# Turned token blocks leave PSUM by two engines, and the overflow list is made later

## What is computed

```
glog = (hf @ w_group + b_group)                    # 4 groups, the best one is taken
elog_sel = ... the 8 logits of that group
top_p, top_i = lax.top_k(jax.nn.softmax(elog_sel, -1), 2)
comb = one_hot weights (token, expert)
a = einsum("nd,edf->nef", hf, w_gate); u = einsum("nd,edf->nef", hf, w_up)
hid = silu(a) * u * comb
y = einsum("nef,efd->nd", hid, w_down)             # w_gate, w_up 1024 x 256, w_down 256 x 1024, all float32
```

## Time and profile before

| | us |
|---|---|
| median of 3 runs | 1248.11 |
| lowest and highest | 1244.79, 1253.91 |
| the profiled execution | 1250.47 |
| span of its instructions | 1248.6 |
| mean granted clock of TensorE | 0.963 |

### The profile page before, as it was taken

One profiled execution on the slowest core, in us unless ns is written; L12 is line 12 of the kernel. 1 busy time (PEld: TensorE's weight loads), 2 busy tenths in 40 slices (PEclk: granted clock), 3 DMA queues, 4 the chain that ended last, 5 costly groups with the idle time before them and its releaser, 6 DMA issues.

```text
span 1248.6 us, 13186 instructions
## 1 busy us (share of the span) xinstructions
PE 1142.8 (92%) x4510; PEld 491.0 (39%) x4510; DVE 477.0 (38%) x1133; ACT 229.1 (18%) x421; POOL 96.1 (8%) x163
## 2 busy tenths in 40 slices
PE   4899999899689999999959999999969999999983
PEld 0444544445433333333335544544643333333331
DVE  0453232226822333333455231334673333333336
ACT  0523220302220000000023332341240000000001
POOL 4000000004210000000030000000420000000000
PEclk9999999998799999999989999999889999999997
DMA  9966548437859999999751322311556999999962
GB/s 375 382 255 248 211 191 331 185 109 269 340 189 400 367 381 377 376 382 392 288 224 38 119 68 101 102 43 76 202 220 258 400 382 392 385 377 382 384 233 84
DMA packets 50087, 328.31 MB, mean 263 GB/s; under 512 B 6144, under 2 KB 7248, under 8 KB 13312
## 3 DMA queue, kind: packets, MB, share of 16 engines
q1 hardware_dynamic: 43520, 299.92, 61.3%
q0 software_dynamic: 4912, 20.95, 4.4%
q10 hardware_dynamic: 1616, 6.93, 1.5%
HBM read 320.90 MB, written 6.88 MB: 263 GB/s over the span
## 4 chain that ended last, share of the span: by engine, by line
PE 80%; DMA 11%; DVE 4%; ACT 2%; issue 2%; SPq 1%; DVEq 0%; PEldq 0%; ACTq 0%
PE bank L647 36%; PE bank L1018 15%; PE bank L1044 11%; PE bank L1035 9%; DMA ring<-in_w_moe 6%; PE bank L668 3%; DMA ring<-in_w_mod 2%; DMA region<-h_store,toki 1%; PE bank L1001 1%; PE bank L1060 1%; PE bank L1027 1%; DMA ring<-in_w_in 1%; DMA ring<-in_w_out 1%; ACT hT L1393 1%; PE bank L1080 1%
## 5 line engine op out<-in xcount | busy, mean ns | idle before, releaser
L1018 PE MATMUL bank<-ring,region 128*64 128x512 f32 x1024 | 236.4, 605 | 5.7 <-issue 5.5
L1044 PE MATMUL bank<-region 128*128 128x512 f32 x384 | 173.3, 601 | 0.0
L647 PE MATMUL bank<-ring,hT 128*128 128x512 f32 x384 | 171.6, 599 | 1.7 <-DMA ring<-in_w_in 1.7
L1018 PEld LDWEIGHTS bank<-ring,region 128*64 128x64 f32 x1024 | 70.3, 138 | 146.6 <-issue 146.6
L1035 PE MATMUL bank<-ring,region 128*64 128x512 f32 x512 | 117.3, 600 | 7.5 <-DMA ring<-in_w_moe 5.6
L1044 PEld LDWEIGHTS bank<-region 128*128 128x128 f32 x384 | 70.3, 190 | 102.5 <-issue 102.5
L647 PEld LDWEIGHTS bank<-ring,hT 128*128 128x128 f32 x384 | 70.9, 190 | 90.5 <-issue 89.9
L2043 DVE TENSOR_TENSOR region<-bank,region 128x512 f32<-128x512 f32 x128 | 82.4, 686 | 47.3 <-PE bank L1035 47.3
L647 PE MATMUL bank<-ring,region 128*128 128x512 f32 x192 | 88.1, 608 | 6.7 <-DMA ring<-in_w_out 3.2
L647 PE MATMUL bank<-hT,ring 128*128 128x384 f32 x256 | 89.2, 500 | 1.3 <-DMA ring<-in_w_in 1.3
L2039 DVE TENSOR_TENSOR region<-region,bank 128x256 f32<-128x256 f32 x32 | 13.5, 421 | 199.8 <-ACT region L1510 199.8
(11 more groups left out here) (301 smaller groups left out, 971.1 us busy)
## 6 DMA issues: line engine op xcount, KB each, us to landing
ring<-in_w_moe SPq DMA_DIRECT2D x201, 1024.0 KB, 9.1
ring<-in_w_mod SPq DMA_DIRECT2D x48, 1024.0 KB, 9.5
ring<-in_w_in SPq DMA_DIRECT2D x24, 1024.0 KB, 7.8
ring<-in_w_out SPq DMA_DIRECT2D x4, 1024.0 KB, 7.5
ring<-in_w_out SPq DMA_DIRECT2D x8, 512.0 KB, 4.2
region<-gate_store POOLq DMA_DIRECT2D x4, 1024.0 KB, 6.6
region<-in_lnrows POOLq DMA_DIRECT2D x4, 1024.0 KB, 8.5
h_store<-region ACTq DMA_DIRECT2D x6, 512.0 KB, 3.3
```

Source lines behind the costliest of these rows:

```text
L647: ins = pe.matmul(out, lhsT, rhs, start=start, stop=stop, skip_group_check=True)
L1018: ins = pe.matmul(bank[6][u * CAP:(u + 1) * CAP, :], xs[:, k, u * CAP:(u + 1) * CAP], ring[:, u, j, at:at + 2 * DE], start=k == 0, stop=k ...
L1044: ins = pe.matmul(bank[2 * t + y][:, :], cwp[:, t * P:(t + 1) * P], ysb[:, min(t, 1), y * HALF:(y + 1) * HALF], start=False, stop=False, s ...
```

## The change

- PE: the group q = 1 of each block goes to bank 6 or 7 (`bank[6 + s % 2]`) instead of a bank of `pj()`. Block 0 waits there for `tok_sb` (all row numbers made, bank 6 free), block 1 for `diag_ready` (bank 7 free), blocks 2 to 5 for the copy of the block two before.
- DVE copies those groups into `xg`, six a layer; ACT keeps the six groups with q = 0 and the four `qrow` copies. The `diag` products no longer have a wait of their own.
- DVE does these copies right behind `diag_ready` (in layer 0 behind `mod_columns`), then `bring_x(0)`, and only then makes the overflow list. In `bring_x(0)` the two register loads now stand ahead of the waits for `xg_ready` and for its own copies.
- PE's product that spreads the list moves from the end of `gather` to behind the up products of pair 0 and its one `add_input`.
- The loop over the overflow experts uses one semaphore for what were two. The order of its work stays.

```diff
@@ gather (PE)
                     for q in range(2):
-                        b = pj()
+                        if q == 0:
+                            b = pj()
+                        else:
+                            b = bank[6 + s % 2]
+                            if s == 0:
+                                pe.wait_ge(S["tok_sb"], (l + 1) * len(ROW_GROUPS))
+                            if s == 1:
+                                pe.wait_ge(S["diag_ready"], l + 1)
+                            if s >= 2:
+                                pe.wait_ge(S["up_free"], l * SC + s - 1)
                         for k in range(4):
                             ins = pe.transpose(b[:, k * P:(k + 1) * P], xrows[s][:, (4 * q + k) * P:(4 * q + k + 1) * P], ident[:, :])
-                        ins.then_inc(S["pj_ready"], 1)
+                        ins.then_inc(S[("pj_ready", "up_ready")[q]], 1)
                     if s == NT - 1:
-                        pe.wait_ge(S["diag_ready"], l + 1)
...
-                pe.wait_ge(S["list_col"], l + 1)
-                pe.matmul(bank[7][:, 0:3 * MAXL], ones[0:MAXL, :], xdiag[:, :, :].rearrange("p a b -> p (a b)"),
-                          start=True, stop=True, skip_group_check=True).then_inc(S["list_row"], 1)
@@ experts (PE)
                 up_first(0)
                 up_second(0)
                 add_input(l, HIDDEN_SUMS)
+                pe.wait_ge(S["list_col"], l + 1)
+                pe.matmul(bank[7][:, 0:3 * MAXL], ones[0:MAXL, :], xdiag[:, :, :].rearrange("p a b -> p (a b)"),
+                          start=True, stop=True, skip_group_check=True).then_inc(S["list_row"], 1)
                 turn_step(0)
...
-                        pe.wait_ge(X[l]["cw"], i + 1)
+                        pe.wait_ge(X[l]["cw"], i * 4 + 4)
@@ ACT
                 for s in range(SC):
-                    for q in range(2):
-                        free(f(xg[:, 4 * q:4 * q + 4, s * P:(s + 1) * P], pj()[:, :].rearrange("p (a c) -> p a c", a=4), ACT.Copy))
+                    free(f(xg[:, 0:4, s * P:(s + 1) * P], pj()[:, :].rearrange("p (a c) -> p a c", a=4), ACT.Copy))
@@ DVE
                 dve.sem_inc(S["diag_ready"], 1)
 
+                if l == 0:
+                    mod_columns(1, 2)
+                for s in range(SC):
+                    dve.wait_ge(S["up_ready"], l * SC + s + 1)
+                    dve.tensor_copy(xg[:, 4:8, s * P:(s + 1) * P], bank[6 + s % 2][:, :].rearrange("p (a c) -> p a c", a=4)).then_inc(S["up_free"], 1)
...
                 def bring_x(i):
                     off = [dve.value_load(offi[0:1, bass.ds(i * G + u, 1)], min_val=0, max_val=NS) for u in range(G)]
+                    if isinstance(i, int) and i == 0:
+                        dve.wait_ge(S["xg_ready"], l + 1)
+                        dve.wait_ge(S["up_free"], (l + 1) * SC)
...
+                bring_x(0)
                 ob = lambda a: a[0:MAXL, :].unsqueeze(1).broadcast_to([MAXL, MAXJ, NE])
...
                 dve.sem_inc(S["list_col"], 1)
 
-                if l == 0:
-                    mod_columns(1, 2)
...
-                dve.wait_ge(S["xg_ready"], l + 1)
-                bring_x(0)
                 dve.wait_ge(S["list_row"], l + 1)
```

More of the change, by code:

```diff
@@ L347, in backbone_step @@
             "fin_state",
-            "h_out", "tok_ps", "tok_sb", "rt_ready", "list_col", "list_row", "gexp_in", "gexp", "assign", "ranks", "slots", "lists", "diag_ready", "xg_ready",
+            "h_out", "tok_ps", "tok_sb", "rt_ready", "list_col", "list_row", "up_ready", "up_free", "gexp_in", "gexp", "assign", "ranks", "slots", "lists", "diag_ready", "xg_ready",
             "cw_ready", "cw_step", "comb_done", "acc_done", "xs_ready", "gu_ready", "sg_ready", "hid_ready", "ht_ready", "ht_sb", "ya_ready", "yb_ready", "ya_sb", "yb_sb",
@@ L358, in backbone_step @@
         landed = [[sem(f"landed{u}_{j}") for j in range(3)] for u in range(G)]
-        X = [{n: sem(f"x{n}{l}") for n in ("l0", "l1", "l2", "xs", "u0", "gu", "sg", "hid", "ht", "hts", "yb", "yas", "ybs", "cw", "ws", "cb")} for l in range(DEPTH)]
+        X = [{n: sem(f"x{n}{l}") for n in ("l0", "l1", "l2", "xs", "u0", "gu", "sg", "hid", "ht", "hts", "yb", "yas", "ybs", "cw", "cb")} for l in range(DEPTH)]
         SMALL = [(small[:, :], A["small"]), (tiny[:, :], A["tiny"])]
@@ L368, in backbone_step @@
         PJ_FRONT = [1, 1]
-        N_PJ_L0 = PJ_FRONT[0] + H * (PJ_HEAD + MV) - MV + 2 * NT + 2 * SC + 4
+        N_PJ_L0 = PJ_FRONT[0] + H * (PJ_HEAD + MV) - MV + 2 * NT + SC + 4
         PJ_END, PJ_QK = [], []
@@ L2067, in pair_weights @@
                     weights(colq[:, bass.ds(i, 1)], S["cw_step"], i * 3 + 3 * p0).then_inc(S["cw_ready"], 1)
-                dve.wait_ge(S["xg_ready"], l + 1)
                 bring_x(0)
+                ob = lambda a: a[0:MAXL, :].unsqueeze(1).broadcast_to([MAXL, MAXJ, NE])
+                more, pos, start, key, pick = xrow
+                own(dve.tensor_tensor(more, ob(cnt), jcap[:, :, :], ALU.is_gt))
+                flat = lambda a: a.rearrange("p a b -> p (a b)")
+                own(dve.memset(xone, 1.0))
+                own(dve.tensor_tensor_scan(flat(pos), xone, flat(more), 0.0, ALU.mult, ALU.add))
+                own(dve.tensor_tensor(key, pos, more, ALU.mult))
+                own(dve.tensor_copy(xcount[:, :], flat(pos)[0:1, MAXJ * NE - 1:MAXJ * NE]))
+                own(dve.tensor_tensor(start, ob(offs), jcap[:, :, :], ALU.add))
+                own(dve.tensor_scalar(start, start, float(-NS), None, ALU.add))
+                for y, what in enumerate((eidx[:, :, :], start, jcap[:, :, :])):
+                    own(dve.scalar_tensor_tensor(out=pick, in0=key, scalar=rank_f[:, 0:1], in1=what, op0=ALU.is_equal, op1=ALU.mult))
+                    own(dve.tensor_reduce(xcol[:, y:y + 1], flat(pick), AX, ALU.add))
+                for y in range(3):
+                    own(dve.tensor_scalar(xdiag[:, y, :], ident[0:MAXL, 0:MAXL], xcol[:, y:y + 1], None, ALU.mult))
+                dve.sem_inc(S["list_col"], 1)
                 dve.wait_ge(S["list_row"], l + 1)
@@ L2105, in _ @@
                         dve.wait_ge(X[l]["cb"], i + 1)
-                        weights(colx[:, bass.ds(i, 1)], X[l]["ws"], i * 3).then_inc(X[l]["cw"], 1)
+                        weights(colx[:, bass.ds(i, 1)], X[l]["cw"], i * 4).then_inc(X[l]["cw"], 1)
                         dve.wait_ge(X[l]["yb"], i + 2)
```

## The result

Six runs of the changed kernel had a median of 1254.58 us (1252.15 to 1255.87), six of the kernel before 1248.42 us (1244.79 to 1253.91). The ratio is 1.0041, 95% interval 1.0021 to 1.0061: slower by 5.1 us (2.6 to 7.6), well inside 1%. A second measurement (`e0_after_again`) gave 1.0028 (1.0009 to 1.0046). So it is a small loss, but a real one, and about 4 us more than the forecast of +0.8.

What follows compares the result with a forecast made beforehand. TensorE, busy in 92% of the span, was taken as the bound, with shifts before and inside each layer's first pair at full value. Layer 0 -1.15 and layer 1 +1.95 gave +0.8 on 1248.1: 1248.9, say 1249 us, range 1242 to 1257.

Steps and rivals of the forecast that it cites:

- Part 1: Transposes of blocks 3 to 5: with four banks PE waits for nobody, 3.4 us instead of 3.95; -0.55 in layer 0.
- part 2: Blocks 1 and 2 and diag products: no change in layer 0; layer 1 stalls for diag_ready, +2.3 us.
- Part 3: Last transpose to first up product: register loads run beside DVE's last block copy; -0.9 us layer 0, -0.65 layer 1.
- Part 4: Up products of pair 0: PE's shorter gap keeps the full clock, -1.7 us in each layer; bounds -1.7 and 0.
- Part 5: Behind pair 0's up products: the list's way through DVE delays the transposes, +2.0 us each layer; bounds 0 and 3.0.
- The clock in the hole: Behind pair 0's up products: the new 2 us PE wait loses the full clock again, +1.7 us each layer.
- slower, by the clock: Rival: the gap before pair 0 still loses full clock, 1252.3 us; with the new wait behind up products 1255.7; chance 0.22.
- two cases in the rows: PE nearly idle from 350 to 353: clock then 0.50; busy 5.90 us in shorter pieces from 630 to 640: stays 1.00.
- The free list: Rival: list's product and copies find room beside silu, costing nothing while the gains stay; 1245 us; chance 0.18.
- The dear copies: Rival: DVE's block copies cost over 1.13 us each, so PE waits for up_free; +4.9, 1253 us; chance 0.04.
- The absorbed shifts: Rival: weights' transfers amid the pairs set the end and PE falls back to them; 1248.1 us; chance 0.10.

Runs made afterwards that it cites:

- e0_after_again: The changed kernel measured once more, unedited, against the kernel before: ratio 1.0028 (1.0009 to 1.0046), +3.5 us.
- e1: Kernel before with only the two register loads of bring_x(0) moved ahead of the wait for xg_ready: ratio 0.9955, -5.6 us.
- e2: Kernel before with only the overflow list moved, DVE code and PE's product at their new places, copies untouched: ratio 1.0040, +5.0 us.
- d1: Kernel before with one edit: the second group of block 1 waits for diag_ready: ratio 1.0022, +2.8 us.
- g1: Kernel before with the two VALUE_SUMS products ahead of pair 0's up products instead of behind its down products: ratio 0.9968, -4.0 us.
- b_combined: Kernel before with register loads ahead of the waits and second groups of blocks 3 and 4 copied by VectorE: 0.9934, -8.3 us; repeated 0.9923, -9.6 us.
- c1: Kernel before with VectorE copying only the second groups of blocks 3 and 4, and the merged overflow semaphore; list and loads unmoved: ratio 0.9966, -4.3 us.
- e6: Changed kernel with the two register loads of bring_x(0) behind its two waits: ratio 1.0047, +5.9 us against the kernel before.
- e3: Changed kernel with blocks 0 and 1 copied wholly by ScalarE, diag_ready awaited only at the diag products: ratio 1.0005, +0.6 us against the kernel before.
- e5: Changed kernel with the two VALUE_SUMS products moved ahead of the transposes of pair 0: ratio 0.9999, -0.1 us against the kernel before.

## Why the prediction was right or wrong

The forecast of no change beyond 1% was right, and the measured time lies in the range, but the +0.8 us was short by about 3 to 4. The range is no strong test: it was drawn around all the rivals, so each of them would have landed in it. By the forecast's own parts:

- **Part 1 was undersized.** Layer 0's turning stage won 1.56 us instead of 0.55. The 24 transposes took 2.81 us, where 3.4 was forecast; the remaining 0.4 came from blocks 1 and 2 and the `diag` products, which part 2 had at 0. The 1.13 us for eight was taken as free of waits, but a row that joins eight covers two banks, and its pace was still that of two banks and one reader; a wait between its halves is the likely rest, though no row shows it by itself. The price of VectorE's copy, 0.69 us, was as assumed (0.7).
- **Part 2 had the right place, and its size by luck.** PE waited for `diag_ready` in layer 1 and not in layer 0, and the total was +2.6 us against +2.3. But from the start of block 1 to the end of the wait it was 4.6 us instead of 3.7, the `diag` products took 3.65 instead of 3.4, and the faster transposes of blocks 3 to 5 (2.81 instead of 3.4) made up for most of it.
- **Part 3 was nearly right.** The loads lie beside the last block copy, but the first token copy came 1.76 us after that copy's start instead of 1.4 in layer 0 (1.51 in layer 1). From the last transpose to the first up product it was 2.66 and 2.42 us instead of 2.3. What the part missed is larger than what it counted: the loads need none of what they stood behind (e1). In the changed kernel they are written behind the last block copy and its wait, so only about half of their time is hidden, although VectorE sits idle for 3.82 us ahead of the fourth block copy. No run has them there.
- **Part 4 failed in layer 1.** "I take it that the clock holds, as in the second: -1.7 in each layer": layer 0 gave -1.7, layer 1 -0.2.
- **Part 5 was right in size** (+2.1 in both layers against +2.0), and e2 measures the list alone at +5.0.
- **The clock in the hole** was left out of the sum and given only to the rival "slower, by the clock". In layer 1 it came: 5.35 instead of 3.65 us, +1.7. From +0.8 to the +3.9 of the traces: the clock in layer 1 +1.5 and +1.7, the turning stage of layer 0 -1.0, small misses of the other terms +0.9.

So the rival on the clock came true for one layer of two. It had 0.22, too little: with bounds of 0 and -1.7 and two cases in the rows, the sum should have taken a value between them. The free list is refuted by e2. The dear copies are refuted by their rows: 0.69 us each, and PE turned blocks 3 to 5 without a wait. The absorbed shifts are refuted by the runs whose two stages alone give the measured difference (e1, d1, g1, b_combined).

No run shares all six blocks while the list and the loads stay where they were, so what the six copies are worth by themselves in the changed kernel isn't measured. Single edits also can't be added up, since several of them win or lose the same clock: c1 and e1 both have the up products back at full clock.

What stays open is what places the clock's fall. The runs give, for the gap ahead of pair 0: after idle times of 1.81 us and less the up products took 7.09 us, 8 of 8 times (e1, g1, b_combined twice, both layers each); after 2.41 to 3.72 us they took 7.09 in 8 cases (layer 0 of the changed kernel, c1 twice, e6's 3.72 among them) and 8.4 to 10.0 in 10 (the kernel before in both layers, layer 1 of the changed kernel, e6's 3.09). But 1.8 us is no safe length: behind the hole, which is 1.80 us in every trace that has it, the down products took 5.35 us in 5 cases of 10 and 3.65 in the other 5 (the changed kernel twice, e2, e3, e6). Ahead of pair 0, in the changed kernel and its variants, it was always layer 1 that lost the clock and layer 0 that kept it, 5 traces each; behind the hole it was layer 1 in the changed kernel twice and in e2, but layer 0 in e3 and e6. The rule of the Trainium skill that the prediction named ("TensorE: Matmul & The Clock Gate", Part 1: The HAM clock gate), a watch that isn't started by the kernel, agrees with gaps of like length that end both ways; that the up products of the same layer came out alike each time is not explained by it.

## What to carry to other kernels

Move register loads and other queue work ahead of the wait that they don't need: two loads moved past one semaphore were the largest gain of a single edit (-5.6 us), since they shorten an idle gap of PE and with it save its clock. Independent work put into such a gap does the same (g1, -4.0; e5). Work taken from an idle stage and put between two links of a chain (here VectorE's way of the list ahead of the hidden product) costs the latency of all that stands between the links (2.1 us in each layer), even if most of its compute is covered. If a copy is shared with a second engine, share first the pieces that meet no signal which isn't there yet: blocks 3 and 4 alone won 4.3 us (c1), while the one wait that sharing block 1 brings cost 2.8 (d1).

## What was not expected of the hardware

- PE's 128x128 transposes at full clock, with nobody to wait for, take 2.81 us for 24, 0.117 each; in groups of eight beside two banks they looked like 0.14.
- VectorE's queue takes 1.5 us (346.9 to 348.4, layer 0) and 1.2 us (933.8 to 935.0, layer 1) for two register loads and their register work, and does them beside the running instruction: in layer 0 of the changed kernel they start at 346.9, at the start of the last block copy.

```profile
L2023 DVEq TENSOR_LOAD <-offi x2: 314/433/552, 346.9 to 347.8; - x2
```

- 2.41 us of idle time cost 1.5 us in the up products by the clock (layer 1 of the changed kernel), while 3.72 us cost them nothing in layer 0 of e6. The hole of 1.80 us cost the down products 1.7 us in 5 cases of 10.
